# The skip term and the order of work in the eight-chunk state-space scan

## What is computed

```python
def ssd_scan(xdt, log_decay, b_in, c_out, init):
    xc, a_cum, bc = _ssd_blocks(xdt, log_decay, b_in)
    cc = c_out.reshape(bc.shape).astype(F32)
    h_in, final = _ssd_chunk_states(xc, a_cum, bc, init)
    ...
    cb = jnp.einsum("bclgn,bcsgn->bgcls", cc, bc.astype(F32))
    y_diag = jnp.einsum("bgcls,bgecls,bcsgep->bclgep", cb, decay_in, xc.astype(F32))
    y_off = jnp.einsum("bclgn,cbgepn,bgecl->bclgep", cc, h_in, jnp.exp(a_cum))
    return (y_diag + y_off).reshape(xdt.shape).astype(xdt.dtype), final
```

## Time and profile before

| | us |
|---|---|
| median of 3 runs | 2534.2 |
| lowest and highest run | 2533.22, 2534.28 |
| the profiled execution | 2533.14 |
| its span, first to last instruction | 2531.3 |
| TensorE busy | 2388.0 (94%) |
| VectorE busy | 1631.4 (64%) |
| ScalarE busy | 940.4 (37%) |
| POOL busy | 276.5 (11%) |

### The profile page before, as it was taken

The page is one execution under the profiler, slowest core; times in us unless marked ns, Lnnn a source line. Parts: engine busy times, 40 slices in busy tenths (PEclk is TensorE's granted clock), DMA queues, the critical chain, the costliest instruction groups (busy, mean ns, idle before and its releaser), DMA issues. The chain is left out here.

```text
span 2531.3 us, 30519 instructions
## 1 busy us (share of the span) xinstructions
PE 2388.0 (94%) x11945; PEld 1927.1 (76%) x11945; DVE 1631.4 (64%) x1685; ACT 940.4 (37%) x1097; POOL 276.5 (11%) x268
## 2 busy tenths in 40 slices
PE   6999899899999999999999999999599999999994
PEld 2468778678877878788787788868588888888882
DVE  7453388633343755324975437578888888888876
ACT  5133311233323533001112000031277777777764
POOL 0000000000143400000000001100012122121210
PEclk9999999999999999999999999999699999999997
DMA  5431154312345313111111115533699999999965
GB/s 203 173 117 42 66 188 171 103 46 84 119 147 156 98 50 108 49 44 50 42 50 38 42 50 179 175 136 117 269 363 362 370 360 363 361 372 387 386 266 204
DMA packets 93966, 437.11 MB, mean 173 GB/s; under 512 B 17432, under 2 KB 28968, under 8 KB 79146
## 3 DMA queue, kind: packets, MB, share of 16 engines
q1 hardware_dynamic: 64714, 349.02, 37.5%
q0 software_dynamic: 29152, 86.69, 9.8%
HBM read 401.12 MB, written 55.51 MB: 180 GB/s over the span
## 5 line engine op out<-in xcount | busy, mean ns | idle before, releaser
L390 PE MATMUL ps<-uT_upper_rest,ring_rest 128*128 128x512 f32 x1280 | 504.7, 394 | 0.0
L390 PE MATMUL ps<-uT_upper_rest,mix_upper 128*128 128x512 f32 x768 | 307.4, 400 | 9.9 <-DVE mix_val L2424 5.3
L390 PE MATMUL ps<-uT_rest,mix_upper 128*128 128x512 f32 x768 | 306.3, 399 | 0.0
L390 PEld LDWEIGHTS ps<-uT_upper_rest,ring_rest 128*128 128x128 f32 x1280 | 240.6, 188 | 61.0
L390 PEld LDWEIGHTS ps<-uT_upper_rest,mix_upper 128*128 128x128 f32 x768 | 145.4, 189 | 47.6 <-DVE mix_val L2424 5.7
L390 PEld LDWEIGHTS ps<-uT_rest,mix_upper 128*128 128x128 f32 x768 | 145.3, 189 | 33.0 <-issue 0.5
L1856 ACT ACTIVATE mix_gates<-ps 128x1024 f32<-128x1024 f32 x24 | 24.7, 1028 | 385.8 <-PE ps L390 368.8
L1907 DVE TENSOR_TENSOR mix_prod<-mix_gates,ps 128x1024 f32<-128x1024 f32 x24 | 29.3, 1221 | 212.4 <-PE ps L390 212.4
L2955 PE MATMUL ps<-ex_u_raw_rest,uT_rest 128*128 128x256 f32 x560 | 157.0, 280 | 0.0
L2953 PE MATMUL ps<-ring_rest,uT_rest 128*128 128x256 f32 (+1 forms) x416 | 135.1, 325 | 3.1 <-DVE uT_rest L3318 2.4
L2953 PE MATMUL ps<-ex_upper,uT_rest 128*128 128x256 f32 (+1 forms) x424 | 134.9, 318 | 0.0
(11 more groups left out here) (477 smaller groups left out, 5502.0 us busy)
## 6 DMA issues: line engine op xcount, KB each, us to landing
sb_spare<-in_ex_g SPq DMA_DIRECT2D x35, 2048.0 KB
ex_u_raw<-in_ex_u SPq DMA_DIRECT2D x35, 2048.0 KB, 10.2
sb_merged<-in_ex_d SPq DMA_DIRECT2D x35, 2048.0 KB
ring<-in_conv SPq DMA_DIRECT2D x32, 512.0 KB, 3.3
ring<-in_w_gate SPq DMA_DIRECT2D x32, 512.0 KB, 3.4
mix_piece<-in_w_late POOLq DMA_DIRECT2D x32, 512.0 KB, 5.4
ring<-in_w_ssd SPq DMA_DIRECT2D x20, 512.0 KB, 3.3
ring<-in_w_mod SPq DMA_DIRECT2D x16, 512.0 KB, 4.5
```

What stands on the lines that cost most here:

```text
L390: last = self.nc.tensor.matmul(out, weight, x[:, k, lo:hi], start=(k == 0 and n == 0), stop=(k == kt - 1 and n == 2))
```

## The change

It has three parts. The identity product `skipped` is dropped, so each diagonal product now starts its own column range in PSUM (`start=True`), and VectorE adds `skip` to `off` before `off` goes to the output, with a semaphore of its own, `skip_added`; POOL may overwrite `skip` when that has happened, and SP loads a new `xs` only when the skip term has been formed from the old one. On VectorE the second half's mix moves ahead of the state's sum, and the read of the last chunk's diagonals moves from behind the first mix to the chunk's beginning. On TensorE the forward product of the next chunk moves behind the last segments and the second diagonal product.

```diff
 # SP
                     sp.wait_ge(diag_mm, 2 * (n - 1))
+                    sp.wait_ge(skip_ready, n - 1)
                     load_xs(sp, n % 2, chunk(n), in_state[n % 2])
 # TensorE
-                def skipped(n, q):
-                    pe.wait_ge(skip_ready, n + 1)
-                    nc.tensor.matmul(ps[:, 3 + q, 0:half], k.const("ident"), skip[:, q * half:(q + 1) * half],
-                                     start=True, stop=False)
...
                         mm = nc.tensor.matmul(ps[:, 3 + q, e * HD:(e + 1) * HD], grow_f[:, n % 2, h, :],
-                                              xs[:, n % 2, h * HD:(h + 1) * HD], start=False, stop=(e == 5))
+                                              xs[:, n % 2, h * HD:(h + 1) * HD], start=True, stop=True)
...
-                    skipped(n, 0)
                     diagonal(n, 0)
                     pe.wait_ge(off_read, 2 * n + 2)
                     if n + 1 < CHUNKS:
...
                         for u in range(3):
                             segments(n + 1, u)
-                        forward_out(n + 1)
-                    skipped(n, 1)
                     if n + 1 < CHUNKS:
                         segments(n + 1, 3)
                     diagonal(n, 1)
+                    if n + 1 < CHUNKS:
+                        forward_out(n + 1)
 # VectorE
                     if n + 1 < CHUNKS:
+                        v.wait_ge(state_done, n + 1)
                         sc.step(tt(by_head(state_b[:, (n + 1) % 2, :]), by_head(state_b[:, n % 2, :]),
                                    per_head(at("total", c, 1)), ALU.mult))
+                    if n:
+                        take_diagonal(n - 1)
                     take_off(n, 0, state_in(c))
                     mix(n, 0)
-                    if n:
-                        take_diagonal(n - 1)
                     if n == 0:
                         v.wait_ge(last_out, 32)
                     take_off(n, 1, off[:, :])
                     v.wait_ge(off_read, 2 * n + 2)
+                    v.wait_ge(skip_ready, n + 1)
+                    tt(off[:, :], off[:, :], skip[:, :], ALU.add).then_inc(skip_added, 1)
+                    v.wait_ge(skip_added, n + 1)
                     tt(state_in(c), state_in(c), off[:, :], ALU.add).then_inc(y_begun, 1)
                     v.wait_ge(y_begun, n + 1)
+                    mix(n, 1)
                     if n + 1 < CHUNKS:
                         v.wait_ge(state_mm, m + 1)
                         after = as_halves(state_b[:, (n + 1) % 2, :])
                         tt(after, after, halves(5), ALU.add).then_inc(state_done, 1)
-                    mix(n, 1)
 # POOL
                     if n:
-                        pool.wait_ge(diag_mm, 2 * n)
+                        pool.wait_ge(skip_added, n)
```

More of the change, by code:

```diff
@@ L1080, in stage_ssd @@
             "grown", "summed", "mixed", "off_read", "state_done", "y_begun", "y_done", "scan_dve"))
-        state_first, out_first = sem("state_first"), sem("out_first")
+        state_first, out_first, skip_added = sem("state_first"), sem("out_first"), sem("skip_added")
         early = [(0, CHUNKS), (1, CHUNKS + 1), (0, CHUNKS + 1), (1, CHUNKS)] + [(0, c) for c in range(CHUNKS - 1)]
```

## The result

| | before | after |
|---|---|---|
| median of 5 runs | 2534.2 us | 2549.8 us |
| lowest, highest | 2530.7, 2539.3 | 2548.2, 2555.9 |
| ratio of the times | | 1.0065, 95% interval 1.0053 to 1.0076 |
| profiled execution's span | 2531.3 us | 2546.4 us |
| VectorE busy | 1631.4 us | 1656.2 us |

The change makes the kernel 0.65% slower, 15.6 us by the medians. The forecast was 2535.2 us, 1.0 above the kernel before, with a range up to 2538.4. Its direction came true, but the loss is far outside the range. For a steady chunk the forecast had even a gain, 0.14 us, and there the sign was wrong too.

A forecast was written before the change was run, and what follows sets the result against it. The prediction took a ring through TensorE and VectorE as the bound; entry -0.4, chunks 1 to 5 -0.7, chunk 6 +1.0 and last chunk +1.05 gave +1.0 us, median 2535.2 us, range 2529.8 to 2538.4.

The forecast's parts named there:

- The new ring: Scan chunk's dependency loop through VectorE and TensorE in the new order: 10.72 us if nothing interferes, against 11.39.
- M: Zero point for times in a chunk: start of the second operation of the first half's mix on VectorE.
- What the change takes away and adds: Per chunk, TensorE loses two skip products (0.75 and 0.65 us); VectorE gains one addition, 0.96 long, 0.99 taken.
- What interferes: In the scan, VectorE operations with two SBUF inputs and POOL operations reading SBUF block each other; observed waits 0.73, 0.60 us.
- VectorE is first by 0.1 us: In a steady chunk VectorE's state scaling asks at 6.69, POOL's skip multiplication at 6.78, so VectorE is served first.
- the price of 0.53 us a chunk: Steady chunk: VectorE's mix waits behind POOL's two multiplications, making 10.72 + 0.53 = 11.25 us.
- the other rivals: Scan alternatives include no contention to speak of (2530.0 us, chance 0.10) and POOL served before the scaling (2537.1, 0.25).
- POOL keeps the port for both multiplications: Rival: VectorE's scaling waits behind both POOL multiplications; chunk 13.04 us, +10.2 in all, 2544.4 us; chance 0.05.
- The clock inside the scan: Rival: TensorE's clock falls within the scan as its load drops to about 79%; several us a chunk; chance 0.02.
- The last diagonal product at the low clock: At the scan's end its twelve records could take up to 1.3 us more; forecast took 0, range kept it.
- The term for the seventh chunk's mix: Chunk 6, no rows left for POOL to load: the second mix waits 1.17 us; chunk 12.42 us, +1.0.
- The first chunk's forecast gain of 0.4: Scan entry: chunk 1 was to start at 819.95 instead of 820.36, -0.4 us.

The follow-up runs named there:

- the kernel with the other form: Changed kernel with VectorE's scaling of the old state written as scalar_tensor_tensor instead of tensor_tensor; one execution of 2552.0 us.
- the kernel with the short multiplications: Changed kernel with POOL's two multiplications a chunk doing one head of twelve from the second chunk on; 2529.1 us, 0.9989 of the kernel before.
- the gap: Changed kernel in which POOL waits for its skip multiplication to complete before starting its second one; 2538.2 us, 1.0024 of the kernel before.

## Why the prediction was wrong

**The new ring** was right. Counted from M = 836.70 the changed kernel has VectorE's operations at 0.87, 1.85, 2.84, 3.84, 4.83 and 5.70 (written: 0.87, 1.86, 2.85, 3.84, 4.83, 5.70), the diagonal product at 5.84 (5.85), the end of the forward product at 8.75 (8.75), the scaling at 6.75 (6.69) and POOL's skip multiplication at 6.77 (6.78). Without the port the chunk was to be 10.72 us, and is 10.65.

**What the change takes away and adds** was right as far as the runs show it: the new addition takes 0.96 us, and the second skip product, put back, 0.65 (857.56 to 858.21). The 0.75 of the first was not measured anew. That the skip term's move alone brings more than the whole change does even without the meetings, 10.36 against 10.65, I had not worked out, since only the sum of the parts was costed.

**What interferes** was right in kind: operations with two inputs in SBUF wait for POOL, others don't.

**The step that failed is "VectorE is first by 0.1 us"**, and with it the price of 0.53 us a chunk. VectorE's scaling was first by 0.02 us in three chunks and later than POOL in the other three, and it was served in none. The lead was a difference of two long sums of terms, each known to some hundredths, and the gain forecast for a chunk stood on it. A second step failed too, which the other rivals shared: behind POOL's first multiplication VectorE didn't get its turn. Together they made the scaling 2.8 us longer and the chunk, at full clock, 13.05 to 13.15 us, where 11.25 was forecast and 10.65 is left without the meetings: 2.4 to 2.5 us a chunk in place of 0.53. The rival "POOL keeps the port for both multiplications" had this, with a chunk of 13.04 us. I gave it 0.05. By its condition it decides only where POOL asks ahead of VectorE, which the rows show in three of the six chunks; in the other three the same happened without it.

**It got 0.05 because of the earlier trace rows**, where VectorE had come in between two such multiplications. The row was read rightly and carried too far. Its pair had come out of a wait (3.27 us for a transfer), and its second multiplication could not have started before 714.87, when its own transfer landed, 0.43 us after VectorE asked. The pair of the new order runs straight on from the load of rows and waits for nothing in between. The first of these differences the change itself made, by taking away the wait for the diagonal product. A row from another stage bears on this one only if the queue ahead of it looks the same.

**The clock inside the scan** had 0.02, on the ground that at 79% load it had stayed up. The load was 76% in a steady chunk (9.87 of 13.05), but it had one piece of idle time of 2.32 us in it (2.42 in most), where the longest from 800 to 810 had been 1.25. The granted clock fell to the lower level for four stretches inside the scan, and the price of one is 1.35 us in the chunk that shows it alone. That the long idle pieces brought it down is not shown: the first stretch (from 817.9) came in a chunk with none over 1.41 us. The last diagonal product at the low clock, which the range held with 1.3 us, cost 1.25.

**The sum with the terms as measured:** against the chunks before, +0.93 for the first, +0.23 for the second, then +1.76, +3.01, +1.66, +1.75, +5.65, and +2.30 for the last: 17.3 us in the scan. The rival's +10.2 and four times 1.35, with 1.25 for the end, make 16.9, but that closeness is partly luck. By the rival's own terms the seventh chunk costs 13.04 + 1.17 - 11.39 = 2.8 us and not the 1.3 in its sum, and the second chunk, for which it had 1.65, cost only 0.23, since it began before the first long scaling was over; the two errors cancel. The term for the seventh chunk's mix, 1.17, was 1.16. The first chunk's forecast gain of 0.4 was hidden by one stretch at the low clock: in the kernel with the other form, whose clock stayed full there, that chunk took 12.54 us, 0.34 less than before the change.

## What to carry to other kernels

When work moves off one engine onto VectorE, list every operation on VectorE with two inputs in SBUF and every POOL operation that reads SBUF, and lay both on one time line: a wait on POOL that looks like a relic may be what keeps them apart, and here one such line was worth 0.65% in the changed kernel and 22 us in the one that only moves the skip term. Where a forecast turns on who asks first by less than 0.1 us, both outcomes should have near even chances: within one kernel the outcome was the same each time, but the lead in the trace didn't tell which. The cheap cure, a wait that makes the order certain, is to be tried with the change. And try the parts alone: the skip term's move gained 0.2% with the old wait and lost 0.65% with the change's own, the mix ahead did nothing, and the forward product last lost 0.6%. The fourth move, the read of the diagonals to the chunk's beginning, was not tried alone.

## What was not expected of the hardware

- An operation's start in the trace is not the moment at which it takes the port. VectorE started 0.02 us ahead of POOL and waited for it (843.45 and 843.47); in the kernel with the short multiplications it started 0.01 ahead and was served (850.37 and 850.38). It isn't chance from chunk to chunk: with a lead of 0.01 to 0.03 us VectorE was served in none of eleven chunks where POOL's multiplication was the long one (three of the changed kernel, four each with the gap and with the other form), and in all four where it was short. Why the length of POOL's work should decide is not shown.
- VectorE can lose the port twice in a row: 3.75 us for an operation of 0.95, behind two multiplications of 1.49 and 1.48. It did so where the pair followed POOL's load directly, and not where the pair had come out of a wait (2.01 and 2.26 us), had a wait inside (2.33), or both (the 2.38 of the earlier trace rows). The Trainium skill, "SBUF — State Buffer", section "Who interferes with whom", has it that the one issued first gets the port for the whole instruction and the other blocks. The exclusion agrees with every row here. The order of issue, as far as the trace shows it, does not at 843.45, and of a waiter against the holder's next instruction the section says nothing. Why the cases differ stays open.
- Such a wait counts as busy. VectorE's busy time rose by 24.8 us over the span, of which the eight new additions are 7.7.
- With one piece of idle time of 2.3 to 2.4 us on TensorE in each, the granted clock came down in some chunks (845.28 to 859.68, 0.88) and not in others (859.68 to 872.73, 1.00).
